# A hybrid decoder layer on one core: inner norms by eight column groups, and the last four V blocks done by token half

## What is computed

```python
mix = hybrid_mixer(x, ...)                       # ... @ w_o
x = layer_norm(DEEPNORM_ALPHA * x + mix, ln1_gain[l], ln1_bias[l])
xa = memory_cross_attention(x, mem, w_mq[l], w_mkv[l], w_mo[l])
x = layer_norm(DEEPNORM_ALPHA * x + xa, ln2_gain[l], ln2_bias[l])
ff = peer_ffn(x, w_pq[l], peer_sub_keys[l], peer_u[l], peer_v[l])
x = layer_norm(DEEPNORM_ALPHA * x + ff, ln3_gain[l], ln3_bias[l])
```

## Time and profile before

| | |
|---|---|
| median of 3 runs | 2392.91 us (2392.11 to 2396.0) |
| the profiled execution, its own time | 2392.88 us |
| its span in the profile | 2391.1 us |
| mean granted TensorE clock | 0.988 |
| TensorE busy | 2310.8 us, 97% |
| VectorE busy | 1678.1 us, 70% |
| `w_o` products end, first norm begins | 608.7 us |
| `w_mo` products end, second norm begins | 841 us |
| U products (experts' activations) | 966 to 1661 us |
| V blocks | 1661 to 2370 us |
| last norm alone | 2370 to 2388 us |

### The profile page before, as it was taken

The page is one execution under the profiler, slowest core; times in us unless marked ns, Lnnn a source line. Parts: engine busy times, 40 slices in busy tenths (PEclk is TensorE's granted clock), DMA queues, the critical chain, the costliest instruction groups (busy, mean ns, idle before and its releaser), DMA issues.

```text
span 2391.1 us, 45242 instructions
## 1 busy us (share of the span) xinstructions
PE 2310.8 (97%) x14770; PEld 2094.6 (88%) x14770; DVE 1678.1 (70%) x2628; ACT 1105.7 (46%) x1716; POOL 635.8 (27%) x425
## 2 busy tenths in 40 slices
PE   7999999999899979999999999999899999999996
PEld 7988799878797879999999999999788888888885
DVE  4444556655643547699999999997677767777556
ACT  4444455543443334344555455554444444444442
POOL 0000000000201020687877778675000000000100
PEclk9999999999899989999999999999999999999998
DMA  8788644565353655688888888887888878888763
GB/s 321 251 277 270 195 140 143 161 224 194 131 184 113 194 141 133 149 196 194 196 197 196 193 197 194 200 196 204 288 288 288 288 245 285 286 285 275 240 220 123
DMA packets 333365, 507.60 MB, mean 212 GB/s; under 512 B 69072, under 2 KB 216784, under 8 KB 325744
## 3 DMA queue, kind: packets, MB, share of 16 engines
q1 hardware_dynamic: 285856, 443.79, 61.3%
q0 software_dynamic: 46736, 62.17, 11.1%
q10 hardware_dynamic: 704, 0.75, 0.1%
HBM read 485.33 MB, written 21.23 MB: 212 GB/s over the span
## 4 chain that ended last, share of the span: by engine, by line
PE 94%; DVE 2%; DMA 1%; ACT 1%; issue 1%; POOL 0%; SPq 0%; DVEq 0%; ACTq 0%; POOLq 0%
PE ps L707 28%; PE ps L670 27%; PE ps L460 18%; PE ps L466 15%; PE ps L660 2%; DMA temps<-gates_scratch 1%; PE ps L608 1%; PE ps L626 1%; DVE split_ring L1221 0%; DMA region<-in_x_dram 0%; PE ps L644 0%; DVE parts L1213 0%; ACT parts L775 0%; ACT split_ring L792 0%; PE ps L539 0%
## 5 line engine op out<-in xcount | busy, mean ns | idle before, releaser
L1221 DVE TENSOR_TENSOR split_ring<-weight_ring,split_ring 128x1024 fp32r<-128x1024 f32 x288 | 353.1, 1233 | 364.7 <-ACT split_ring L792 356.6
L707 PE MATMUL ps<-parts,temp_parts 128*128 128x512 f32 x2304 | 545.5, 390 | 6.3 <-DVE parts L1570 6.2
L1164 POOL DMA_INDIRECT gates_scratch<-sb_gains x256 | 506.6, 1979 | 158.3 <-issue 100.4
L707 PEld LDWEIGHTS ps<-parts,temp_parts 128*128 128x128 f32 x2304 | 433.2, 188 | 98.2 <-DVE parts L1570 8.1
L670 PE MATMUL ps<-parts,u_hi 128*128 128x240 f32 x3904 | 477.1, 275 | 0.0
L792 ACT ACTIVATE split_ring<-weight_ring 128x1024 fp32r<-128x1024 f32 x288 | 302.8, 1059 | 367.1 <-PE ps L460 226.1
L670 PEld LDWEIGHTS ps<-parts,u_hi 128*128 128x128 f32 x3904 | 456.0, 188 | 0.0
L460 PE MATMUL ps<-split_ring,parts 128*128 128x512 f32 x1920 | 439.8, 391 | 5.6 <-DVE parts L1337 3.9
L460 PEld LDWEIGHTS ps<-split_ring,parts 128*128 128x128 f32 x1920 | 360.7, 188 | 81.0 <-DVE split_ring L1221 4.1
L977 ACT ACTIVATE u_hi<-u_turned 128x1024 fp32r<-128x1024 f32 x244 | 259.0, 1062 | 316.8 <-DVE u_turned L1428 256.3
L466 PE MATMUL ps<-parts,split_ring 128*128 128x256 f32 x3072 | 379.5, 286 | 12.4 <-DVE split_ring L1221 7.1
(11 more groups left out here) (222 smaller groups left out, 1409.4 us busy)
## 6 DMA issues: line engine op xcount, KB each, us to landing
u_raw<-in_peer_u_dram SPq DMA_DIRECT2D x1024, 128.0 KB
region<-in_peer_v_dram SPq DMA_DIRECT2D x256, 512.0 KB, 4.7
weight_ring<-in_w_in_dram SPq DMA_DIRECT2D x96, 512.0 KB, 5.1
weight_ring<-in_w_mkv_dram SPq DMA_DIRECT2D x64, 512.0 KB, 4.1
gates_scratch<-temps POOLq DMA_DIRECT2D x16, 1024.0 KB, 7.2
weight_ring<-in_w_o_dram SPq DMA_DIRECT2D x32, 512.0 KB, 4.3
weight_ring<-in_w_mq_dram SPq DMA_DIRECT2D x32, 512.0 KB, 3.7
weight_ring<-in_w_mo_dram SPq DMA_DIRECT2D x32, 512.0 KB, 3.7
```

The lines of the kernel that those rows point to most:

```text
L707: m = nc.tensor.matmul(ps[:, 4 * t + q, :], e[:, c], v, start=first and n == 0, stop=False, skip_group_check=True)
L1164: pool.indirect_dma_start(gates_by_one, bass.IndirectOffsetOnAxis(ap=idx_all[:, j:j + 1], axis=0), gate_all[:, j:j + 1], None, compute_op= ...
L1221: nc.vector.tensor_tensor(w_lo[j % SPLIT], raw[j % RAW], w_hi[j % SPLIT].bitcast(F32), ALU.subtract).then_inc(lo_ready, 1)
```

## The change

**Inner norms.** The norm is done by eight groups of 256 columns, as the transposes go. In `norm` VectorE runs gain and bias of group g+1, then the `lo` of group g itself, from PSUM (`turned_lo`), and between them the `split_lo` of slices 4 to 7 of the next pair. GpSimd keeps only the power. ScalarE copies a group once to `hi` (in the second norm also to `xw`, one group late) and splits slices 4 to 7 between the groups. On TensorE each turned group is followed by the slice that needs it. The residual is two instructions of 512 and not one of 1024, and the `split_lo` of the panel's last slice is moved behind group 0's `lo`. SyncE's wait ahead of the nine DMAs of x2 is for all eight groups, as it was for all four chunks.

**End.** `hi` and `lo` of E and V of blocks 124 to 127 get buffers of their own (`held_v`, where the E of used blocks lay; `held_e` in the temporaries), so their splits wait for no product. The fold is done ahead of block 124. TensorE then does t=0 of all four blocks (48 matmuls), counts `row_done`, and does t=1 quarter by quarter (12 matmuls each), counting each. In the last norm VectorE starts t=0 at the first count; for t=1 it takes each quarter as it is counted. GpSimd clears the pads of the eight held E tiles ahead of its loads of the last gain and bias.

TensorE's and VectorE's parts, cut:

```diff
             for g in range(8):
-                if g % chunks == 0:
-                    pe.wait_ge(x_ready, first_chunk + g // 2 + chunks // 2)
-                turn(src, g, nth + g)
-                if g in (3, 7):
-                    pe.wait_ge(turned_lo_ready, nth - 16 + g // 2 + 1)
-                    slices("cols", range(g // 2 - 1, g // 2 + 1), pair, acts, 0, 1)
...
+            turn_group(0)
+            for g in range(8):
+                if g == 0:
+                    turn_group(1)
+                pe.wait_ge(turned_taken, nth + g + 1)
+                slices("cols", [g], pair, acts, 0, 1)
+                if g + 2 < 8:
+                    turn_group(g + 2)
...
-            last_block(NKEY - 1, 1)
+            pe.wait_ge(pad_set, 2)
+            for i in range(FREE_V, NKEY):
+                pe.wait_ge(e_lo_ready, i + 1)
+                for q in range(4):
+                    pe.wait_ge(v_lo_ready, i * 4 + (q + 1))
+                    m = held_product(0, q, i)
+            m.then_inc(row_done, 1)
+            for q in range(4):
+                for i in range(FREE_V, NKEY):
+                    m = held_product(1, q, i)
+                m.then_inc(row_done, 1)
...
+                normalize(0)
+                for g in range(8):
+                    if g < 7:
+                        normalize(g + 1)
+                    turned_lo((p1, p3), turned_before, [g])
+                    if g == 0:
+                        split_lo(pair - 1, [PS + 3])
+                    if 3 <= g < 7:
+                        split_lo(pair, [g + 1])
...
-                dve.wait_ge(v_used, NKEY * 4 - 2 + 2 * t)
                 if t == 0:
+                    dve.wait_ge(row_done, 1)
                     dve.wait_ge(x2_landed, 256)
                 chunk = [slice(q * BANK, (q + 1) * BANK) for q in range(NP)]
-                for q in range(NP + 1):
+                for q in range(NP if t else 0):
+                    dve.wait_ge(row_done, 2 + q)
+                    steps.did(nc.vector.scalar_tensor_tensor(out=y_out[:, t, chunk[q]], in0=x2_back[:, t, chunk[q]], scalar=ALPHA,
+                                                             in1=ps[:, 4 * t + q, :], op0=ALU.mult, op1=ALU.add))
+                    steps.wait()
+                    steps.did(nc.vector.bn_stats(stats[:, t, q, :], y_out[:, t, chunk[q]]))
```

More of the change, by code:

```diff
@@ L890, in _ @@
                 split_pair(pair)
-            copy_turned_whole(p1, 16, whole)
-            section("cols", r0, MQ0, NP // 2, 2 * BANK)
+            copy_turned_norm(16, MQ0)
+            for i in range(NP // 2):
+                split_pair(i + MQ0, lambda s: take("cols", r0, (i * 2 + s) * 2 * BANK, i + MQ0, s, 2 * s),
+                           first=4 if i else 8)
             for h in range(MH):
@@ L1035, in v_parts @@
                     v_part(i, pair, b, q)
-                    if q == 1 and not last:
+                    if q == 1:
                         expert_parts(i + 1, 1 - b)
```

206 lines of the change are left out of this document (123 added, 83 removed).

## The result

The changed kernel takes 2372.4 us at the median of six runs (2368.4 to 2379.2), the kernel before 2393.5 (2392.1 to 2398.0): a ratio of 0.9911 with a 95% interval of 0.9895 to 0.9927. In a later comparison it took 2374.3 against 2393.8, 0.9919 (0.9906 to 0.9933). The forecast was 2371.9, and the profiled execution's span is 2369.5 against the 2370.1 of the sum. What follows compares the two profiled executions, spans 2369.5 and 2391.1, so 21.6 us.

The account below looks back on a forecast made before the run. TensorE, busy 97% of the span, bounds the kernel, so gains where it idles or at the end arrive whole: 3.55 + 9.5 + 7.9 = 20.95 us, from 2392.9 to 2371.9 us, range 2366.5 to 2378.5.

Parts of the forecast that it names:

- First norm: First inner norm: slice 0 starts at about 617.0, eight slices end at 645.3 instead of 648.9; gain 3.55 us.
- the clock: Both inner norms: 4.8 us of slices at half speed, so 2.4 us lost, bounds 1.8 to 2.9.
- Second norm: Second inner norm: slice 0 starts at 849.45 instead of 859.26, eight slices end at 877.75; gain 9.5 us.
- rival (a): Second norm: VectorE leads because 128-column pieces cost what 256 ones cost; 2.3 us lost, 2374.2; chance 0.10.
- SyncE's margin: Second norm: w_pq loads queued behind the x2 stores still bring slice 12 in time, margin 5 us, cost nothing.
- End: Last norm: VectorE starts 8.2 us earlier, after t=0, and never waits again; gain 7.9 us, bounds 5 and 8.2.
- The held parts: Held V blocks at the end: block 127's last rest ready at about 2355, needed at 2358.5; margin 3.5 us.
- (c): Held V loads come late, 8 us to land instead of 4.7: 2375.0; chance 0.05.
- (e): The end's gain fails since t=0 can't run alone; given nothing.
- The V stage's loads: V stage: gain and bias loads go out some 9 us later; zero effect, bounds 1 us gain, 4 us loss.
- Rival (b): V stage: gate and V loads fall worse, one more pair of waits of 6.2 us: 2378.1; chance 0.09.
- rival (d): Inner norms: clock stays at 1.2 GHz; 2395.4 in one norm (chance 0.02), 2418.9 in both (0.03).

Follow-up runs that it names:

- the norms alone: The kernel before with only the edits to the two inner norms, without the held V blocks: 2378.0 us, 0.9928 of before.
- the end alone, loads first: The kernel before with only the held V blocks and the new last norm, gain and bias loads issued ahead of the pads: 2385.2 us, 0.9966.
- loads-first run: The changed kernel with the last norm's gain and bias loads issued ahead of the wait for lines and the pads' clearing: 2367.8 us, 0.9893.

## Why the prediction was right, and where it was not

**What bounds it, and the sum.** Right. That a gain at one of the three places arrives at the end whole held for each within what the timed runs can tell (the norms alone 15.1 us, with an interval of 13.4 to 20.8 that holds the 16.7 of the trace, and the end alone, loads first, 8.6), but not for what is won after them: 2.1 us more in the second norm are lost in the V stage's start.

**First norm: 3.55 us, bounds 2.5 to 4.6; it was 5.8.** The mechanism was right and the term mis-sized by 2.3 us, outside its bounds. Three of its steps: the clock (2.4 us taken as lost; slice 1 starts at 621.24, 4.41 us behind slice 0, against a period of 3.31, so 1.1), 1.3 us; the start (617.0 - 608.86 = 8.14 us, measured 7.46), 0.7, of which 0.26 is the power, which took 0.89 us rather than 1.15; the period (3.36, measured 3.31), 0.3 over the six steps that have transposes. I had carried the clock's rise over from the kernel before as a time from slice 0, with only half a microsecond of doubt. It came 2.5 us behind slice 0 in one norm and 5.0 in the other, with nearly the same work of TensorE ahead of both.

**Second norm: 9.5 us, bounds 7.5 and 10.8; it was 10.9**, 0.1 over the upper bound. The start is 7.49 us behind the residual where 849.45 - 841.07 = 8.38 was forecast, 0.4 of it the power, which took 0.73 us; the period gave 0.3 more. The forecast took the power's 1.15 us from the first norm, though the kernel before shows 0.88 us for it in the second (845.33). And the start of slice 0 was to gain 9.8 us against 4.2 in the first norm, so 2.3 times as much, not three times. Here the clock was about as assumed (slice 0 to slice 1 5.51 us, 2.2 lost). A piece of 128 columns follows the next at 0.26 us ((1.13 - 0.35) / 3), forecast 0.27, so rival (a) fell: no slice waits for VectorE. The Trainium skill, "VectorE: DVE Perf Modes", section "The TRN2 errata", prefers tiles of at least 512 elements; here the pieces of 128 elements cost 0.26 us each where 128 elements of the 512 ones cost 0.17, and that was under the slack: the trace shows no wait for it. SyncE's margin held too: 0.53 us for each load of `w_pq`, and no wait for slice 12.

**End: 7.9 us; it was 7.8.** Each step held: VectorE's start 10.85 us before TensorE's end (10.87), t=1 behind t=0 at once, VectorE at 9.95 us behind TensorE. The held parts are in time: the last rest ends at 2342.04, and the last of t=0's products need it at about 2344.8, 2.8 us later (3.5 forecast). Rivals (c) and (e) fell: 96 held products run in a row without a wait; that two blocks instead of four cost 5.4 us shows the step's arithmetic from the other side.

**The V stage's loads: 0, with 4 us of loss as a bound; it was 2.6 us of loss.** This step failed, within its bounds. The sentence named the right thing, that gain and bias go out later and that "their collision with the V loads moves with them", and gave it nothing. It does not just move: put off by the wait for the lines and the pads, they stand with the first loads of x, and the load of gates behind them takes 11.09 us where a block takes 5.44. The loads-first run took the wait away (and 3.9 us off the V stage), and four buffers for the gates did it without moving them. The Trainium skill, "DMA: Bandwidth & Descriptors", section "SWDGE vs HWDGE vs iDMA", says that GpSimd's DMAs and those of the other engines feed different internal queues of a DMA engine, which serves them in turn. The trace agrees in so far as the 120 KB on SyncE's queue took 11.09 us while GpSimd's 2 MB were in flight for most of that time (7.6 and 10.7 us from issue to landing); in what order a DMA engine served them no row shows. Rival (b), at 6.2 us, had the mechanism near, at over twice its size.

**The clock, rival (d).** It did not come: in the slices the clock is full from 619.3 and 848.0 on, with four transposes between each two slices, at a period of 3.31 us. The Trainium skill, "TensorE: Matmul & The Clock Gate", section "A second HAM failure mode", describes a kernel with short idles between groups; here TensorE has none between groups, and the trace shows no going back and forth.

The terms that were off stood on opposite sides (2.3 and 1.4 us more in the norms, 2.6 less in the V stage, 0.5 for the later start), so that 21.6 us against 20.95 is a better sum than its parts: that they cancelled was luck.

## What to carry to other kernels

Where an instruction is put ahead of others on a queue that also issues loads, price each load behind it at its new place, beside what is in flight then: here three lines cost 4 us by the profile (3.9 in the V stage), and 5 by the timed medians, of a gain of 25. And a forecast of the clock's rise should be bounded from zero to the longest seen, not by half a microsecond around the one row at hand. A gain ahead of a stage that starts on loads is worth only what the loads allow; ask when they land before paying for it.

## What the runs showed of the hardware

- With the same code and the same waits, the granted clock behind a wait of 1.8 to 3 us of TensorE fell to 0.50 in some runs and stayed full in others; ahead of the first norm this is worth up to 5 us from run to run.
- Extra matmuls over an idle stretch kept the clock full in one norm (24 of them, 2.84 us, then gaps of 0.59 and 1.19 us). In the other (36 of them, 4.09 us, gaps of 1.04 and 0.93) it fell at the end of the second gap, as group 1 was turned, and stayed down until 618.9:

```profile
616.00:619.00 3.00, 3.00 (x16) 0.51 0.16 30
```

- GpSimd's power on 128x2 elements, with nothing changed in it, took 1.15 us in the first norm and 0.88 in the second in the three kernels with the old norms, and 0.88 to 0.89 and 0.73 to 0.75 in the eleven with the new ones. What VectorE does beside it is what differs; whether that is the cause no run shows.
- A load of 120 KB took 11.09 us beside two of 1 MB and two of 128 KB, 7.81 when it went out 5 us behind the same two of 1 MB, and 4.3 at the median of the whole profile; the V loads of 512 KB ran beside it each time.
- At the start of the V stage, beside GpSimd's eight loads of 128 KB and its first picked lines, a V load of 512 KB took 13.2 and 14.2 us to land, against 4.6 at the median of those two profiles. Issued 1.04 us earlier, it landed at the same time.
